# Second feed-forward product of a decoder block as seven half products of sums (Strassen) in seven of eight groups

## The reference

```python
def reference(x, norm_mix, w_in, ..., w_out, norm_mlp, w_ff1, w_ff2):
    ...
    for l in range(DEPTH):
        h = _rmsnorm(x, norm_mix[l])
        proj = h @ w_in[l]
        ...
        merged = (jax.nn.sigmoid(g_sb) * (o_sb @ w_branch_sb[l])
                  + jax.nn.sigmoid(g_sa) * (o_sa @ w_branch_sa[l]))
        x = x + merged @ w_out[l]
        h2 = _rmsnorm(x, norm_mlp[l])
        x = x + jnp.square(jax.nn.relu(h2 @ w_ff1[l])) @ w_ff2[l]
    return x
```

## Time and profile before

| | |
|---|---|
| median of 3 runs | 782.08 us (781.05 to 782.23) |
| the profiled execution: time | 780.9 us |
| the profiled execution: span of the trace | 779.2 us |
| mean granted TensorE clock | 0.998 of full speed |
| PE busy, share of the span | 97% (3566 matmuls) |
| DVE, ACT, POOL busy | 51%, 39%, 17% |
| DMA, mean over the span | 91 GB/s, 70.63 MB |

### The profile page before, as it was taken

The page is one execution under the profiler, slowest core; times in us unless marked ns, Lnnn a source line. Parts: engine busy times, 40 slices in busy tenths (PEclk is TensorE's granted clock), DMA queues, the critical chain, the costliest instruction groups (busy, mean ns, idle before and its releaser), DMA issues.

```text
span 779.2 us, 9155 instructions
## 1 busy us (share of the span) xinstructions
PE 753.8 (97%) x3566; PEld 596.9 (77%) x3566; DVE 395.9 (51%) x585; ACT 303.6 (39%) x419; POOL 131.1 (17%) x144
## 2 busy tenths in 40 slices
PE   8999899999997999899998999999999999999998
PEld 4768688777875555588887888888888888888886
DVE  5344887688797856455655432233332333233331
ACT  5235552455564676643223442114311242114310
POOL 2104326000002454003301111002200120002100
PEclk9999999999999999999999999999999999999999
DMA  9208231401011212113090223332233213332011
GB/s 333 108 14 242 83 109 61 136 21 54 8 49 54 55 55 55 54 61 131 25 326 25 83 80 109 109 109 69 94 109 108 107 62 106 103 108 94 14 54 54
DMA packets 47989, 70.63 MB, mean 91 GB/s; under 512 B 2642, under 2 KB 27218, under 8 KB 47955
## 3 DMA queue, kind: packets, MB, share of 16 engines
q1 hardware_dynamic: 47954, 70.17, 27.4%
HBM read 65.71 MB, written 2.10 MB: 87 GB/s over the span
## 4 chain that ended last, share of the span: by engine, by line
PE 88%; DVE 6%; ACT 3%; issue 1%; POOL 1%; DMA 0%; SPq 0%; DVEq 0%; ACTq 0%; POOLq 0%
PE ps L393 13%; PE ps L395 13%; PE ps L394 13%; PE ps L386 13%; PE ps L388 12%; PE ps L387 12%; PE ps L1256 2%; PE ps L1292 2%; PE ps L1333 1%; DVE cut_lo L377 1%; PE ps L1238 1%; PE ps L1323 1%; PE ps L1268 1%; PE ps L1117 1%; PE ps L1252 1%
## 5 line engine op out<-in xcount | busy, mean ns | idle before, releaser
L393 PE MATMUL ps<-cut_hi,a_hi 128*128 128x512 f32 x480 | 189.6, 395 | 0.8 <-DVE a_lo L822 0.8
L395 PE MATMUL ps<-cut_hi,a_lo 128*128 128x512 f32 x480 | 187.2, 390 | 0.0
L394 PE MATMUL ps<-cut_lo,a_hi 128*128 128x512 f32 x480 | 187.0, 389 | 0.0
L386 PE MATMUL ps<-b_hi,cut_hi 128*128 128x512 f32 (+1 forms) x336 | 127.5, 379 | 0.0
L387 PE MATMUL ps<-b_lo,cut_hi 128*128 128x512 f32 (+1 forms) x336 | 127.3, 379 | 0.0
L388 PE MATMUL ps<-b_hi,cut_lo 128*128 128x512 f32 (+1 forms) x336 | 127.3, 379 | 0.0
L393 PEld LDWEIGHTS ps<-cut_hi,a_hi 128*128 128x128 f32 x480 | 90.3, 188 | 19.5 <-DVE a_lo L822 1.3
L395 PEld LDWEIGHTS ps<-cut_hi,a_lo 128*128 128x128 f32 x480 | 90.1, 188 | 19.2
L377 DVE TENSOR_TENSOR cut_lo<-raw,cut_hi 128x2048 fp32r<-128x2048 f32 (+1 forms) x38 | 76.8, 2022 | 53.1 <-ACT cut_hi L355 53.0
L394 PEld LDWEIGHTS ps<-cut_lo,a_hi 128*128 128x128 f32 x480 | 90.2, 188 | 17.6
L370 DVE TENSOR_TENSOR cut_lo<-raw,cut_hi 128x2048 fp32r<-128x2048 f32 x24 | 55.0, 2292 | 83.5 <-ACT cut_hi L364 83.5
(11 more groups left out here) (141 smaller groups left out, 888.5 us busy)
## 6 DMA issues: line engine op xcount, KB each, us to landing
raw<-in_w_ff_dram SPq DMA_DIRECT2D x32, 1024.0 KB, 5.4
raw<-in_w_in_dram SPq DMA_DIRECT2D x16, 1024.0 KB, 5.3
gates<-in_x_dram SPq DMA_DIRECT2D x8, 512.0 KB, 5.8
raw<-in_w_out_dram SPq DMA_DIRECT2D x4, 1024.0 KB, 4.9
raw<-in_w_in_dram SPq DMA_DIRECT2D x4, 512.0 KB, 6.2
raw<-in_w_branch_sb_dram SPq DMA_DIRECT2D x2, 1024.0 KB, 5.0
raw<-in_w_branch_sa_dram SPq DMA_DIRECT2D x4, 512.0 KB, 6.0
out_dram<-gates SPq DMA_DIRECT2D x8, 256.0 KB, 2.0
```

Source lines behind the costliest of these rows:

```text
L386: nc.tensor.matmul(dst, w_hi, rhs_hi, start=start, stop=False)
L393: nc.tensor.matmul(dst, l_hi, w_hi, start=start, stop=False)
L394: nc.tensor.matmul(dst, l_hi, w_lo, start=False, stop=False)
L395: return nc.tensor.matmul(dst, l_lo, w_hi, start=False, stop=stop)
```

## The change

The second product is made group by group in 2 x 2 blocks. A group now has 512 hidden features (`FG` = 8). With H the hidden values of a group, tokens in halves of 256 and features in halves of 256 (`h11`, `h12`, `h21`, `h22`, each 128 x 2 x 256), and B the rows of `w_ff2`, output columns in halves of 512 (`b11` to `b22`, each 128 x 2 x 512), the first seven groups use seven block products in place of eight. The left sides are H11, S2 = S1 - H11, H12, S1 = H21 + H22, S4 = H12 - S2, S3 = H11 - H21 and H22. The right sides, in this order, are B11, t2 = B22 - t1, B21, t1 = B12 - B11, B22, t3 = B22 - B12 and t4 = B21 - t2. A product is named by its left side (A11, S2, A12, S1, S4, S3, A22). Each is 2 tiles of 128 tokens, 2 k, 3 matmuls: 12 matmuls of 512 columns. Products that share an output are run on in the same bank and added to `xres` or to `zsum` after each step, since later outputs hold the sums of earlier ones; in the end `zsum` is added to three of the four blocks (`add_z`). The last group (`for u in range(8)` on PE) is made as eight usual tiles of 12 matmuls.

Around this, what the engines do per group:

- PE: `pe_round(g)` has the four chunks of the first product for group g+1 between the seven products of group g.
- ACT: relu of four chunks, the high parts of seven left sides (`left_high`) and seven right sides (`right_high`, 128x1024 each), and of two `w_ff1` slabs (`f_high`).
- DVE: four squares, the low parts of seven right sides (`right_low`) and two `w_ff1` slabs (`f_low`), four sums t1 to t4 of 128x1024, and 14 additions of a bank (`drain`).
- POOL: four sums S1 to S4 of 128x512 and the low parts of seven left sides (`left_low`).
- SP: two slabs of `w_ff1` and two of `w_ff2` per group, as before 1 MB each; the second of `w_ff2` (B21 and B22) is loaded when the right side B22 of the group before has been cut (`r_lo` 7g+5).

The diff, cut to its core:

```diff
-FG = 4
+FG = 8
+A11, S2, A12, S1, S4, S3, A22 = range(7)
+HI = [A11, A12, S1, S2, S3, S4, A22]
...
+        home = [home3[j] for j in (1, 2, 0, 1, 2, 0, 2)]
...
+            def load_round(g, f0=True, rest=True):
+                if f0:
+                    sp.wait_ge(f_lo, 2 * g + 3)
+                    load_f(g + 2, 0)
+                if rest:
+                    sp.wait_ge(r_lo, 7 * g + 1)
+                    load_w(g + 1, 0)
+                    if f0:
+                        sp.wait_ge(f_lo, 2 * g + 4)
+                        load_f(g + 2, 1)
+                    sp.wait_ge(r_lo, 7 * g + 5)
+                    load_w(g + 1, 1)
...
-            with pool.Fori(0, FG) as g:
-                for c in range(KD):
-                    pool.wait_ge(f1_hi, 8 * g + c + 1)
-                    pool.tensor_tensor(a_lo[:, c, :], ff_sq[c % 2], a_hi[:, c, :].bitcast(F32),
-                                       ALU.subtract).then_inc(f1_cut, 1)
+            def left_parts(g, first=False):
...
+                pool.wait_ge(f1_sq, 4 * g + 4)
+                pool.tensor_tensor(sum_of[S1], h21, h22, ALU.add).then_inc(s_made, 1)
+                left_low(g, A11)
+                pool.wait_ge(s_made, 4 * g + 1)
+                pool.tensor_tensor(sum_of[S2], sum_of[S1], h11, ALU.subtract).then_inc(s_made, 1)
+                left_low(g, S2)
+                pool.tensor_tensor(sum_of[S3], h11, h21, ALU.subtract).then_inc(s_made, 1)
+                pool.wait_ge(s_made, 4 * g + 2)
+                pool.tensor_tensor(sum_of[S4], h12, sum_of[S2], ALU.subtract).then_inc(s_made, 1)
+                for q in (A12, S1, S4, S3, A22):
+                    left_low(g, q)
...
+            def relu(n, c, first=False):
+                act.wait_ge(f1_done, 4 * n + c + 1)
+                if not first:
+                    act.wait_ge(s_made, 4 * (n - 1) + (3 if c % 2 == 0 else 4))
+                    act.wait_ge(l_lo, 7 * (n - 1) + (1 if c % 2 == 0 else 7))
+                A(hid[:, c, :], bank(6 + c % 2), ACT.Relu).then_inc(f1_relu, 1)
...
+            def act_last_end(g):
+                last_high(0)
+                last_high(1)
+                hidden_high(1)
+                right_high(g, S3)
+                last_high(2)
+                relu(g + 1, 2)
...
+            def dve_round(g, first=False):
+                right_low(g, S2)
+                right_low(g, A12)
+                square(g + 1, 0)
+                drain(g, A11, first)
+                drain(g, S2, first)
+                right_low(g, S1)
+                t4_made(g)
+                f_low(g + 1, 1)
+                right_low(g, S4)
+                square(g + 1, 1)
+                drain(g, A12, first)
+                right_low(g, S3)
+                drain(g, S1, first)
+            def dve_round_end(g, first=False):
+                f_low(g + 2, 0)
+                t1_t3(g + 1)
+                square(g + 1, 2)
+                drain(g, S4, first)
+                right_low(g, A22)
+                drain(g, S3, first)
+                t2_made(g + 1)
+                right_low(g + 1, A11)
+                square(g + 1, 3)
+                drain(g, A22, first)
...
+            def product(g, q, first=False):
+                hi, lo = home[q]
+                pe.wait_ge(r_lo, 7 * g + q + 1)
+                pe.wait_ge(l_lo, 7 * g + q + 1)
...
+                for t in range(2):
+                    if not (first and back):
+                        pe.wait_ge(drained, 14 * (g + back) + 2 * before + t + 1)
+                    for j in range(2):
...
+                        T.matmul(dst, l_h, hi[:, j, :], start=opens and j == 0, stop=False, skip_group_check=True)
+                        T.matmul(dst, l_h, lo[:, j, :], start=False, stop=False, skip_group_check=True)
+                        mm = T.matmul(dst, l_l, hi[:, j, :], start=False, stop=(j == 1), skip_group_check=True)
+                    mm.then_inc(prod_done, 1)
+            def pe_round(g, first=False):
+                ff1(g + 1, 0)
+                product(g, A11, first)
+                product(g, S2, first)
+                ff1(g + 1, 1)
+                product(g, A12, first)
+                product(g, S1, first)
+                ff1(g + 1, 2)
+                product(g, S4, first)
+                product(g, S3, first)
+                ff1(g + 1, 3)
+                product(g, A22, first)
```

More of the change, by code:

```diff
@@ L450, in _ @@
                 sp.dma_start(xres[:, m, :], x_d[m * P:(m + 1) * P, :]).then_inc(x2_in[m], 16)
[L451 to L468, removed]
+            def load_f(n, half):
+                j = (SL_FF + half) % RAW
+                sp.dma_start(raw[:, j, :].rearrange("p (k c) -> p k c", k=8),
+                             wf1[:, bass.ds(512 * n + 256 * half, 256)].rearrange("(k p) c -> p k c", p=P)
+                             ).then_inc(raw_in[j], 16)
@@ new lines, in left_high @@
+            def left_high(n, q, first=False):
+                if q in (A11, A12, A22):
+                    act.wait_ge(f1_sq, 4 * n + 4)
+                else:
+                    act.wait_ge(s_made, 4 * n + q_made[q])
+                if not first:
+                    act.wait_ge(prod_done, prod_end(n - 1, q))
+                A(left_hi[:, q], left[q], ACT.Copy).then_inc(l_hi, 1)
+            q_made = {S1: 1, S2: 2, S3: 3, S4: 4}
+            t_turn = {S1: 1, S3: 2, S2: 3, A22: 4}
+            home_of = {A11: (-1, S1), S2: (-1, A22), A12: (-1, S3), S1: (0, A11), S4: (0, S2), S3: (0, A12), A22: (0, S4)}
@@ new lines, in right_high @@
+            def right_high(g, q, first=False):
+                if q in (A11, A12, S4):
+                    act.wait_ge(*ff_arrived(2 if q == A11 else 3, g))
+                else:
+                    act.wait_ge(t_made, 4 * g + t_turn[q])
+                if first and q in (A11, A12):
+                    act.wait_ge(f1_done, 2)
+                elif not (first and q == S2):
+                    back, user = home_of[q]
+                    act.wait_ge(prod_done, prod_end(g + back, user))
+                A(home[q][0], right[q], ACT.Copy).then_inc(r_hi, 1)
@@ new lines, in add_z @@
+            def add_z(m, n, drains):
+                for t in range(2):
+                    dve.wait_ge(drained, drains + t + 1)
+                    part = xres[:, m + t, n * 512:(n + 1) * 512]
+                    V.tensor_tensor(part, part, zsum[t], ALU.add).then_inc(z_added, 1)
+            f_low(0, 1)
+            square(0, 0)
+            square(0, 1)
+            t1_t3(0, first=True)
+            t2_made(0, first=True)
+            f_low(1, 0)
+            square(0, 2)
+            right_low(0, A11)
@@ new lines, in _ @@
+            pe_round(0, first=True)
+            with pe.Fori(1, FG - 1) as g:
+                pe_round(g)
+            held = 14 * (FG - 2)
+            for u in range(8):
+                n, m = divmod(u, TB)
+                dst = bank(LAST_BANK[u])
+                if u in (4, 5):
+                    pe.wait_ge(f1_sq, 4 * (FG - 1) + u - 1)
+                else:
+                    pe.wait_ge(drained, held + 2 * {0: A12, 2: A22, 4: S4}[LAST_BANK[u] // 2 * 2] + u % 2 + 1)
+                for c in range(4):
+                    if u == 0:
+                        pe.wait_ge(hid_lo, c + 1)
+                    if c < 2:
+                        pe.wait_ge(last_lo, 2 * n + c + 1)
+                    l_h, l_l = (part[:, c, m // 2, m % 2 * P:m % 2 * P + P] for part in (left_hi, left_lo))
+                    hi, lo = (w[:, c // 2, :] for w in home_last[2 * n + c % 2])
+                    T.matmul(dst, l_h, hi, start=(c == 0), stop=False)
+                    T.matmul(dst, l_h, lo, start=False, stop=False)
+                    mm = T.matmul(dst, l_l, hi, start=False, stop=(c == 3))
+                mm.then_inc(last_done, 1)
```

391 lines of the change are left out of this document (264 added, 127 removed).

## The result

The change makes the kernel faster: 769.55 us (median of 4 runs, 768.71 to 770.28) against 781.61 us (4 runs, 781.05 to 782.23) for the kernel before, a ratio of 0.985 [0.983, 0.986]. Forecast were 768.8 us, within 762.5 to 776. The profiled execution took 768.7 us, its span is 766.9 us; forecast for it were 767.7. The other three executions took 0.8 to 1.6 us longer than it and list a mean granted clock of 0.993, where it has 0.996.

A forecast was written before the change was run, and what follows sets the result against it. In the feed-forward part PE never idles, so time is matmuls times 0.2267 us. For the profiled execution 780.9 - 19.0 + 5.8 = 767.7 us, or 768.8 against the median; range 762.5 to 776.

The forecast's parts named there:

- Taken away: Second product, seven groups: 84 matmuls fewer at 0.2267 us each, 19.0 us saved, all on PE's path.
- POOL on split sources: POOL operations on sources split in two runs of 256: 1.29 us taken as lower bound, 1.47 as upper, giving 771.8.
- dearer: Rival: POOL takes 1.47 to 1.55 us on split sources; at 1.55 steady rounds wait 0.4 each, 775.8 us; chance 0.18.
- slower: Rival: DVE and POOL queue bounds every round, PE waiting before product S4 for additions for S1; 787.8 us, chance 0.04.
- DVE beside POOL: Where a DVE operation with two SBUF sources meets one of POOL's, one stands still: 1.15 us per meeting.
- Walk through a steady round: DVE, POOL and PE followed through one round: slack 2.8 us at product S4, so a steady round costs nothing.
- (a) Round 0: No product A22 in front: left S2 late by 0.3 us, the slab for ff1(1,2) by 0.2.
- (b) The last round: Last Strassen round: ACT's right S3 stands behind the last `w_ff2` slab's load; PE waits 4.4 us before S4.
- (c) The last group: Fourth left part: square(7,3) stands behind four `add_z` on DVE; hidden low part ready 0.9 us after PE wants it.
- The sum of waits: PE's waits in round 0, the last Strassen round and the last group: 0.3 + 0.2 + 4.4 + 0.9 = 5.8 us.
- A granted clock below 1: Listed, without a size, among the signs that would show the forecast wrong.
- The median: Whole kernel: 768.8 us for the median, against 767.7 for the profiled execution.

The follow-up runs named there:

- matmuls_back: Changed kernel with the first matmul of each of the 28 chunks behind group 0 made three times more, 84 in all: 785.72 us, ratio to before 1.006.
- all_waits_out: Changed kernel with ACT's right S3 ahead of the last slab wait, round 0's right S2 cut earlier, square(7,3) ahead of the last add_z: 762.77 us.
- warm_matmuls: Changed kernel with 19 bf16 matmuls of zeros ahead of product S4 in the last Strassen round, where PE waits: 768.63 us, ratio to before 0.984.
- three_more_dve: Changed kernel with three more 512-wide, two-SBUF-source DVE operations per round between t4 and the slab: 776.03 us, ratio to before 0.993.
- s3_first: Changed kernel with ACT making right side S3 before it waits for the last slab, in the last Strassen round: 763.97 us, ratio to before 0.978.
- six_more_dve: Changed kernel with six more 512-wide, two-SBUF-source DVE operations per round between t4 and the slab: 797.33 us, ratio to before 1.022.

## Why the prediction was right

- **Taken away**: 84 matmuls at 0.2267 us. Right; matmuls_back and all_waits_out bear out count and price on both sides. The 216 ns that the Trainium skill gives for such a matmul (VectorE: DVE Perf Modes, section on the TRN2 errata) was not the price: at 18.1 us saved the part could not go below 319.0, and in all_waits_out it took 318.6. The bf16 matmuls of zeros in warm_matmuls do start 0.216 us apart (trace, 722.89 to 726.56); the fp32r ones never came closer than 0.2267.
- **POOL on split sources**, the unknown price: the lower bound, 1.29 us, holds (L617, 1.295). With it fell "dearer" and, as things were, "slower". (The forecast's waits at 1.47 add up to 8.7, not 8.8.)
- **DVE beside POOL**: forecast 1.15 us per meeting, measured 1.09 on DVE where it queues behind a whole POOL operation (2.30 against 1.21), always with operations that read two SBUF sources; right A12, which starts 0.4 us before POOL's record ends, loses 0.26. By the rule in the Trainium skill (SBUF — State Buffer, section "SBUF: two separate sides") the port is held for the whole instruction. With POOL's full 1.29 for each meeting the forecast would have been 1.0 us higher; 1.09 was added. Whether the port is held for less than POOL's record lasts, or shared, these traces do not tell.
- **Walk through a steady round**: each step on DVE and POOL within 0.15 us, and no wait. But the forecast looked for the tightest place at product S4 (2.8 us slack); for work added ahead of the slab it is ff1(g+1,2), with 2.1 (three_more_dve).
- **(a) Round 0**: 0.3 for left S2, measured 0.5. The 0.2 for the slab of ff1(1,2) did not come in this trace; in that of s3_first, whose round 0 is the same, it is there (0.18 at 472.3).
- **(b) The last round**: each link of the chain came as put, at 24.6, 29.8, 32.4, 33.8 and 34.4 for forecast 24.5, 29.6, 32.2, 33.6 and 34.3; wait 4.6 for 4.4. s3_first shows it by taking the chain away.
- **(c) The last group**: 0.9 forecast, nothing seen. It was there, under cover: 0.6 in warm_matmuls, 1.1 in s3_first, 0.5 in all_waits_out even with the square moved up.
- **The sum of waits**, 5.8 forecast and 6.7 measured: the missing term is the clock. "A granted clock below 1" stood under what would be wrong, and it came for seven matmuls, 1.5 us. In warm_matmuls, where it is kept up, the part loses 6.0 us (324.0 against 318.0), close to the 5.8. So the forecast is 1.0 us short of the profiled execution (767.7 against 768.7): a cost of 1.5 was left out and S4's wait was 0.2 too small, while a wait of 0.9 was counted that this cost hid. That the two errors nearly cancel is luck, not insight into the clock.
- **The median**, 768.8 forecast and 769.55 measured: the forecast put it 1.15 us above the profiled execution, as before the change; it came 0.85 above. The other three executions list the lower mean clock, 0.993, so their slow stretch was probably longer than 1.5 us, perhaps like the 2.9 of three_more_dve. They have no trace, so this is not shown; it would also explain why s3_first is 5.6 us faster by the medians and 4.8 by the traces.
- **The slower rival** was priced without the clock. six_more_dve shows that repeated waits can cost half as much again, 22 us of waits and 12 of slow matmuls, so that it would have begun earlier than at 19 us of waits.

## What to carry to other kernels

Walk through one round with durations taken beside the other engine, then walk through the first and the last round as well: there the neighbours differ, and an in-order queue may hold a step whose data is ready behind a load that has not landed. Where the walk gives PE an idle time of several microseconds, add some slow matmuls behind it; and before a removed wait is counted as won, ask what it hid.

## What was not expected of the hardware

The granted clock of TensorE fell to half for a short while after idle times inside a stretch of full work. After 4.4 us idle it was 0.50 for 7 matmuls (1.5 us lost), after 5.3 us 0.51 for 14 (2.9 us), both in the last round. After 2.6 us in matmuls_back it stayed at 1.00, as after 2.5 us at S4 in six_more_dve and after 0.8 to 1.7 us elsewhere. After the 2.1 us waits of six_more_dve, which came once in a round, it fell in four rounds and stayed up in the fifth. So the length of the wait alone does not decide it. What decides between these was not tried. That PE's idle time is what starts it is shown by warm_matmuls alone.
